# A hybrid decoder step on one Trainium2 core: u laid out by transfers inside the chip in stage 1, the state recurrence on GpSimd

## The chip, the cores and the metric

The kernel runs on one core of a Trainium2 chip. A core has TensorE (PE: matrix products and transposes, into PSUM), VectorE (DVE), ScalarE (ACT), GpSimd (POOL) and SyncE (SP); each runs its own list of instructions and waits for the others by semaphores. SyncE, ScalarE and GpSimd can issue transfers (DMA). The metric is the device time of the kernel in microseconds.

## The reference, cut to what matters

One step of a one-layer decoder on 256 prompt tokens and 8 x 8 sample tokens (NT = 320), width 2048. It has an attention branch, a state space branch (S5) with 64 groups of 16 channels and 64 complex states, gates that merge them, and a feed-forward part. What bears on the change:

```python
z = _rmsnorm(x, g_mix) @ w_in                       # columns: q 1024, kv 1536, gt 48, u 1024, mg 4096
# the S5 branch, per group of 16 channels of u
xr = jnp.einsum('btgc,gpc->btgp', uf, bbr)
xi = jnp.einsum('btgc,gpc->btgp', uf, bbi)
# h[t] = a * h[t-1] + x[t], a and h complex, started with h0 for the samples and 0 for the prompt
_, _, hr, hi = lax.associative_scan(_cplx_affine_combine, (a_r, a_i, xr, xi), axis=1)
y = (jnp.einsum('btgp,gcp->btgc', hr, c_re) - jnp.einsum('btgp,gcp->btgc', hi, c_im)
     + d_skip.reshape(SSM_NGROUPS, SSM_GROUP) * uf)
```

All is float32. The large products are made of three: each operand is split into a rounded part (hi) and the rest (lo), and hi x hi, hi x lo and lo x hi are added.

## The kernel before, in words

The kernel is a row of programs, each a list for every engine, with a barrier between them (`program`, L141).

**Stage 1** (L377 to L595) makes q, kv, gt and u. Weights come in tiles of 128 columns (1 MB): SyncE loads (`load_tile`, L231), ScalarE rounds (`round_tile`, L245), VectorE subtracts (`rest_tile`, L252), TensorE multiplies (`multiply`, L259, 48 matmuls of 320 columns), and VectorE scales the result into its place (`scale_in`, L555). The order is q (8 tiles), kv (12), gt (one, in two halves), u (8). GpSimd only loads a few small tables (L400 to L409). `uT` has channels on partitions and tokens along a row, and lies in `oT`.

**Stage 2** (L764 to L1241) is the S5 branch, with time cut into chunks of L = 8 tokens: 40 chunks, 32 of the prompt and 8 of the samples. Between its pieces lie the *dense steps*, the function `D` of each engine (L647 to L703): half a tile (8 blocks of 128 rows) of the gate columns mg, 24 matmuls on TensorE, with a load and a rounding on ScalarE (L629), a subtraction on VectorE (L633) and, every second time, a scaled copy out (`gate_out`, L641) and its store. 48 of them belong to this stage. `half_load` n reuses one of three buffers, rounding n one of two, so ScalarE may round step n + 1 when TensorE has finished step n − 1. By hand, TensorE's order is:

1. 24 transposes of u (L854), their copies to `un` (VectorE L1065, ScalarE L990), three stores to DRAM (`u_dram`, L778) and loads back as rows of chunks (L784). SyncE and ScalarE issue the parameter loads before (L769 to L774, L985 to L995).
2. 9 dense steps, between which VectorE makes the powers of a (L1110 to L1122), Bbar (L1127 to L1132) and the copies of C and h0 (L1139, L1142). Small transposes stand between them (L860, L869, L878).
3. The pair loop over 32 pairs of groups (L914): `spread_pair` on VectorE (L1147) makes `EB` for pair m + 3; GpSimd copies u of one pair (L828); `turn_pair` transposes EB (L894) and u (L896); ScalarE copies both (L1014, L1015); `multiply_pair` (L907) makes the chunk inputs `ea`, which VectorE copies (L1166). A dense step after every second pair. At m = 12 and 20 VectorE builds a table Q (`make_q`, L1169).
4. `taps` of parts 0 and 1 (L934), whose results ScalarE copies (`keep_taps`), and 8 dense steps, while VectorE runs the recurrence: `state_step` (L1208), five small operations, 31 times for the 31 chunk borders, and then the final states. TensorE waits for `h_done` (L965).
5. Eight parts of four pairs: `outputs_of` (L949, L956), two dense steps, `taps(part + 2)`. VectorE makes Q for part + 2 between its two dense steps. GpSimd adds the diagonal (L840, L845); SyncE then spreads the taps into a block matrix T by eight transfers inside the chip (`spread_g`, L787), which `outputs_of` reads, and stores the outputs. T must have been cleared by GpSimd (L832).
6. The final states are transposed and stored (L977, L978).

The stages behind (attention with the last 8 gate tiles, samples, merge and feed-forward) are not touched, but for where a few buffers lie.

## Time and profile before

| | us |
|---|---|
| three runs | 2180.3, 2175.05, 2174.73 |
| median | 2175.05 |
| the profiled execution | 2175.88 |
| its span, first to last instruction | 2174.1 |

In that execution TensorE is busy for 2053.7 us (94%), VectorE for 1071.0 (49%), ScalarE for 799.9 (37%) and GpSimd for 114.7 (5%). The busy time of TensorE is modelled for its pipelined matmuls, so a full stretch is not proof of full use, but an empty one is proof of the opposite. Its clock, where nothing lowers it, is 2.4 GHz, shown as 1.00; the mean of the span is 0.977. In a row of the trace the number in front is the start in microseconds from the start of the span, the second the duration, and brackets hold the idle time of that engine before the operation and what ended it.

### The profile page before, as it was taken

The page shows a single profiled execution, that of the slowest core. Times are in us where ns is not written, and L with a number is a line of the kernel's source. Part 1 is how long each engine was busy: PE and PEld are TensorE (multiplying, and loading weights), DVE is VectorE, ACT ScalarE, POOL GpSimd, SP SyncE. Part 2 cuts the span into 40 slices and gives each one's busy share as a digit, 9 for nine tenths or more (in the row PEclk, how much of TensorE's full clock was granted, in tenths as well). Part 3 has the DMA queues.
Part 4 walks back from the last instruction along what each step waited for, and adds up shares of the span by engine and source line. Part 5 has one row for each costly group of instructions (what it writes and reads, how often), then busy time and mean ns, then how long its engine had stood idle before and what let it go on. Part 6 is the DMA issues. An engine that isn't in the chain of part 4 may idle for free.

```text
span 2174.1 us, 39080 instructions
## 1 busy us (share of the span) xinstructions
PE 2053.7 (94%) x15964; PEld 1924.6 (89%) x15964; DVE 1071.0 (49%) x1725; ACT 799.9 (37%) x1132; POOL 114.7 (5%) x173
## 2 busy tenths in 40 slices
PE   8999798898897888899999999999999999999997
PEld 6999787787885555599999999999999999999996
DVE  4433487774563344545554444444444444444443
ACT  5222232343343455654434333223322333233344
POOL 1000011000000212200001000000000000000011
PEclk9999898999997999999999999999999999999999
DMA  7645543455356988745645445455545554554443
GB/s 184 201 135 155 136 123 98 124 147 155 90 162 252 375 313 330 284 151 172 213 139 153 142 148 155 133 160 152 154 132 158 155 149 128 154 168 144 140 134 115
DMA packets 554452, 364.74 MB, mean 168 GB/s; under 512 B 68913, under 2 KB 529666, under 8 KB 553506
## 3 DMA queue, kind: packets, MB, share of 16 engines
q1 hardware_dynamic: 472530, 314.00, 47.0%
q10 hardware_dynamic: 80096, 41.25, 7.1%
q0 software_dynamic: 1712, 7.97, 1.1%
q8 instruction: 72, 1.18, 0.2%
q14 instruction: 42, 0.34, 0.0%
HBM read 345.45 MB, written 23.63 MB: 170 GB/s over the span
## 4 chain that ended last, share of the span: by engine, by line
PE 56%; issue 6%; SPq 2%; DMA 1%; DVE 1%; ACT 1%; POOL 1%; POOLq 0%; DVEq 0%; ACTq 0%
PE bank L279 55%; SPq L1284 1%; SPq L1285 1%; DMA arena<-in_cache_kv_dram 0%; POOL ysT L1733 0%; DMA xT<-out_dram 0%; DVE w_lo L255 0%; PE bank L1866 0%; PE bank L1841 0%; ACT w_hi L250 0%; PE bank L2082 0%; PE bank L1832 0%; POOL arena L1743 0%; DVE rstd L2596 0%; PE bank L1800 0%
## 5 line engine op out<-in xcount | busy, mean ns | idle before, releaser
L279 PE MATMUL bank<-hx,w_hi 128*128 128x320 f32 x3072 | 676.3, 309 | 1.5 <-DVE w_lo L255 1.5
L255 DVE TENSOR_TENSOR w_lo<-w_raw,w_hi 128x2048 fp32r<-128x2048 f32 (+2 forms) x222 | 464.0, 2090 | 345.6 <-ACT w_hi L250 345.5
L279 PE MATMUL bank<-act,w_hi 128*128 128x320 f32 x2432 | 537.0, 310 | 3.2 <-DVE w_lo L255 2.4
L279 PEld LDWEIGHTS bank<-hx,w_hi 128*128 128x128 f32 x3072 | 513.8, 188 | 1.9 <-issue 1.8
L250 ACT CAST w_hi<-w_raw 128x2048 fp32r<-128x2048 f32 (+2 forms) x222 | 385.5, 1737 | 318.3 <-PE bank L279 314.4
L279 PE MATMUL bank<-hx,w_lo 128*128 128x320 f32 x1536 | 474.6, 309 | 0.0
L279 PEld LDWEIGHTS bank<-act,w_hi 128*128 128x128 f32 x2432 | 406.0, 188 | 4.6 <-DVE w_lo L255 3.1
L279 PE MATMUL bank<-act,w_lo 128*128 128x320 f32 x1216 | 375.8, 309 | 0.0
L279 PEld LDWEIGHTS bank<-hx,w_lo 128*128 128x128 f32 x1536 | 288.3, 188 | 0.0
L662 PE MATMUL bank<-actr,half_hi 128*128 128x320 f32 x1024 | 239.9, 323 | 20.6 <-DVE half_lo L633 20.3
L279 PEld LDWEIGHTS bank<-act,w_lo 128*128 128x128 f32 x1216 | 228.3, 188 | 0.0
L662 PEld LDWEIGHTS bank<-actr,half_hi 128*128 128x128 f32 x1024 | 176.5, 196 | 28.6 <-DVE half_lo L633 25.9
L279 PE MATMUL bank<-actr,w_hi 128*128 128x320 f32 x896 | 197.4, 309 | 1.2 <-DVE arena L565 1.2
L662 PE MATMUL bank<-actr,half_lo 128*128 128x320 f32 x512 | 162.1, 317 | 0.0
L279 PEld LDWEIGHTS bank<-actr,w_hi 128*128 128x128 f32 x896 | 149.9, 188 | 1.6 <-DVE arena L565 1.5
L279 PE MATMUL bank<-actr,w_lo 128*128 128x320 f32 x448 | 138.4, 309 | 0.0
L633 DVE TENSOR_TENSOR half_lo<-half_raw,half_hi 128x1024 fp32r<-128x1024 f32 x64 | 78.1, 1220 | 66.5 <-ACT half_hi L629 66.2
L629 ACT CAST half_hi<-half_raw 128x1024 fp32r<-128x1024 f32 x64 | 66.8, 1045 | 119.3 <-PE bank L662 70.5
L2329 ACT CAST act<-arena 128x320 fp32r<-128x320 f32 x44 | 20.2, 459 | 231.0 <-DVE arena L2612 231.0
L662 PEld LDWEIGHTS bank<-actr,half_lo 128*128 128x128 f32 x512 | 100.0, 195 | 0.0
L2326 ACT ACTIVATE cst<-arena 128x320 f32<-128x320 f32 x44 | 20.8, 472 | 191.2 <-DVEq L2604 191.2
L279 PEld LDWEIGHTS bank<-actr,w_lo 128*128 128x128 f32 x448 | 84.1, 188 | 0.0
(395 smaller groups left out, 1777.2 us busy)
## 6 DMA issues: line engine op xcount, KB each, us to landing
arena<-in_cache_kv_dram SPq DMA_DIRECT2D x120, 512.0 KB, 7.1
w_raw<-in_w_gate_dram SPq DMA_DIRECT2D x44, 1024.0 KB, 5.1
w_raw<-in_w_up_dram SPq DMA_DIRECT2D x44, 1024.0 KB, 5.1
w_raw<-in_w_down_dram SPq DMA_DIRECT2D x64, 704.0 KB, 4.7
half_raw<-in_w_in_dram ACTq DMA_DIRECT2D x64, 512.0 KB, 4.5
w_raw<-in_w_in_dram SPq DMA_DIRECT2D x20, 1024.0 KB, 5.1
w_raw<-in_w_glu_dram SPq DMA_DIRECT2D x32, 512.0 KB, 5.0
w_raw<-in_w_out_dram SPq DMA_DIRECT2D x16, 1024.0 KB, 5.8
```

Of the source, the lines that this page charges most:

```text
L250: nc.scalar.copy(w_hi[s][:, 0:job.kt * job.width], raw[s][:, 0:job.kt * job.width]).then_inc(S(f"hi_ready{s}"), 1)
L255: nc.vector.tensor_tensor(w_lo[s][:, 0:job.kt * job.width], raw[s][:, 0:job.kt * job.width], w_hi[s][:, 0:job.kt * job.width].bitcast(F32) ...
L279: mm = pe.matmul(bank[:, 0:NT], w[s][:, at:at + P], x[:, kk, :], start=first and k == 0 and m == 0, stop=final and k == job.kt - 1 and m == 2)
L629: nc.scalar.copy(half_hi[n % 2][:, :], raw3[n % 3][:, :]).then_inc(S("w_rounded"), 1)
L633: nc.vector.tensor_tensor(half_lo[n % 2][:, :], raw3[n % 3][:, :], half_hi[n % 2][:, :].bitcast(F32), ALU.subtract).then_inc(S("w_split"), 1)
L662: mm = pe.matmul(PS[t % 2][:, 0:NT], w[h][:, k * P:(k + 1) * P], actr[:, x, 8 * h + k, :], start=h == 0 and k == 0 and m == 0, stop=h == 1 ...
L1284: at = sp.value_load(ptab[0:1, n:n + 1], min_val=0, max_val=n_pool - 1)
L1285: sp.dma_start(dst, page_rows[bass.ds(at, 1), :, :].rearrange("o t n -> (o t) n")).then_inc(S(landed), 16)
L2326: A.activation(sB[0], tg, ACT.Silu).then_inc(S("silu_ready"), 1)
L2329: A.copy(actr[:, 0, i, :], tmp).then_inc(S("hid_rounded"), 1)
```

## The change

- In stage 1 u comes before kv and gt. Its scaled copy puts the tokens of a chunk position together (`u_in`). When u is complete, GpSimd issues 64 transfers from `uT` to `UTa_flat` (now in `ysT`), 16 partitions x 8 x 40 elements each. The transposes of u, `un`, the stores and loads by `u_dram`, GpSimd's copies (L828), the transposes at L896 and the copies at L1014 are gone.
- The first three half loads and all parameter loads of stage 2 are issued at the end of stage 1, and waited for there.
- In stage 2 the small transposes come first, six dense steps precede the pair loop (of these, VectorE handles three between the first three `spread_pair`). ScalarE makes the copies of C and h0. The powers are made in three rounds of 1, 2 and 4; Bbar for 8 pairs before the loop, for 24 at its start.
- In the pair loop ScalarE copies the products (`copy_pair`), two pairs late.
- The recurrence is on GpSimd (`scan_steps`), for 16 pairs at a time: all 31 steps of the first half from pair 16 of the loop on, the second half in pieces of 11, 11 and 9 steps behind the diagonals of parts 1, 2 and 3. TensorE waits for `h_done` before part 0 and before part 4.
- Dense steps: 6, then 16 in the loop, 4 before the parts, and 3, 3, 3, 3, 3, 3, 2, 2 in the parts (`PART_D`).
- The final states of the samples are made on VectorE in part 2.

```diff
-                for n, job in enumerate((job_q[1], job_kv, job_gt, job_u)):
+                for n, job in enumerate((job_q[1], job_u, job_gt, job_kv)):
...
+                for n in range(3):
+                    half_load(sp, gates, n)
...
+                taps_in = UTa_flat.rearrange("p (t g h a) -> p t g h a", t=8, g=4, h=2)
+                for j in range(8):
+                    for s in range(L):
+                        pool.dma_start(taps_in[s * CH:(s + 1) * CH, :, j // 2, j % 2, :],
+                                       uT[j * CH:(j + 1) * CH, :, s * NCH:(s + 1) * NCH]).then_inc(S("u_spread"), 16)
+                pool.wait_ge(S("u_spread"), 64 * 16)
...
-                for m in range(GH):
-                    part = m // PG
-                    if m % PG == 0:
-                        pool.wait_ge(S(f"u_landed{part % 2}"), 16 * (part // 2 + 1))
...
+                def scan_steps(half, first, last):
+
+                    gs = slice(half * HG, (half + 1) * HG)
+                    a8r = PK[:, 0, L, gs].unsqueeze(1).broadcast_to([P, 2, HG])
+                    for n in range(first, last):
+                        state, extra = Ha[:, n, :, gs], ea[:, n, :, gs]
+                        G.tensor_tensor(sc[:, 1, 0, gs], NPI[:, L, gs], state[:, 1, :], ALU.mult)
+                        G.tensor_tensor(sc[:, 1, 1, gs], PK[:, 1, L, gs], state[:, 0, :], ALU.mult)
+                        scan_link(G.tensor_tensor(sc[:, 0, :, gs], a8r, state, ALU.mult))
+                        scan_link(G.tensor_tensor(sc[:, 2, :, gs], sc[:, 0, :, gs], extra, ALU.add))
+                        out = Ha[:, n + 1, :, gs] if n < SCAN else FinP[:, :, gs]
+                        scan_link(G.tensor_tensor(out, sc[:, 2, :, gs], sc[:, 1, :, gs], ALU.add))
+
+                pool.wait_ge(S("h_zero"), 1)
+                pool.wait_ge(S("powers_ready"), 1)
+                pool.wait_ge(S("e_copied"), HG)
+                scan_steps(0, 0, SCAN)
+                pool.sem_inc(S("h_done"), 1)
                 pool.wait_ge(S("eb_ready"), GH)
                 for b in range(2):
                     nc.gpsimd.memset(Tt[b], 0.0).then_inc(S("t_zero"), 1)
...
+                    if part == 1:
+                        pool.wait_ge(S("e_copied"), GH)
+                    if 1 <= part < 4:
+                        scan_steps(1, STEPS[part], STEPS[part + 1])
...
-                for _ in range(8):
+                for _ in range(4):
                     D()
-                pe.wait_ge(S("h_done"), 1)
                 for part in range(NPART):
+                    if part % 4 == 0:
+                        pe.wait_ge(S("h_done"), part // 4 + 1)
                     outputs_of(part)
-                    D()
-                    D()
+                    for _ in range(PART_D[part]):
+                        D()
...
-                    nc.scalar.copy(UTa[:, m, :], PS[4 + m % 2][:, 256:336])
                     nc.scalar.copy(stg[m % 2], PS[4 + m % 2][:, 0:256]).then_inc(S("e_staged"), 1)
+                    if m >= 2:
+                        copy_pair(m - 2)
                     if m % 2:
                         D()
...
                 for part in range(NPART):
-                    D()
-                    if part + 2 < NPART:
-                        make_q(part + 2)
-                    D()
+                    for n in range(PART_D[part]):
+                        D()
+                        if n == 0 and part + 2 < NPART:
+                            make_q(part + 2)
```

## Rows read from the trace of the kernel before

**Rows 1.** Stages by time: busy us of each engine, clock, DMA share, GB/s.
```profile
236.40:290.50 54.10, 42.48 (x264) 40.48 (x265) 36.52 (x122) 15.43 (x19) 0.77 (x2) 0.87 0.76 184
290.50:389.10 98.60, 91.50 (x746) 81.75 (x744) 71.86 (x187) 30.79 (x80) 16.66 (x34) 0.91 0.40 108
389.10:438.00 48.90, 38.66 (x330) 35.02 (x330) 41.92 (x180) 13.41 (x28) 1.98 (x6) 1.00 0.44 116
438.00:511.50 73.50, 72.31 (x832) 64.78 (x836) 47.51 (x63) 32.74 (x88) 5.36 (x16) 1.00 0.58 149
```

**Rows 2.** TensorE in order of time, start of stage 2: start, duration, operation, idle before.
```profile
236.49 4.04 PE L854 MATMUL bank<-cst,oT 128*128 128x128 f32 x20 [2.36 <-PEq L148]
...
249.32 0.90 PE L662 MATMUL bank<-actr,half_hi 128*128 128x320 f32 x2 [4.46 <-DVE half_lo L633]
```

**Rows 3.** VectorE in order of time, around the parameter chain.
```profile
256.71 0.25 DVE L1073 COPY xT<-bank 128x96 f32<-128x96 f32 x1
...
263.21 0.49 DVE L641 TENSOR_TENSOR sq<-bank,rstd 128x320 f32<-128x320 f32 x1
```

**Rows 4.** TensorE in order of time, one turn of the pair loop.
```profile
310.92 0.38 PE L894 MATMUL bank<-cst,ysT 128*128 128x128 f32 x2
311.24 0.31 PE L896 MATMUL bank<-cst,arena 40*128 40x40 f32 x2
311.48 0.44 PE L907 MATMUL bank<-arena,ysT 128*64 128x40 f32 x8
...
312.83 0.56 PE L662 MATMUL bank<-actr,half_hi 128*128 128x320 f32 x2
...
316.45 0.38 PE L894 MATMUL bank<-cst,ysT 128*128 128x128 f32 x2
```

**Rows 5.** VectorE's groups in stage 2: operation, count, busy us, mean ns, idle before.
```profile
L633 DVE TENSOR_TENSOR half_lo<-half_raw,half_hi 128x1024 fp32r<-128x1024 f32 x48 | 58.5, 1218 | 33.4 <-ACT half_hi L629 33.1 <-DVE oT L1230 0.2
L1158 DVE TENSOR_TENSOR arena<-arena 128x256 f32<-128x256 f32 x32 | 13.9, 434 | 0.0
L641 DVE TENSOR_TENSOR sq<-bank,rstd 128x320 f32<-128x320 f32 x24 | 11.6, 484 | 7.6 <-PE bank L662 7.4
...
L1186 DVE TENSOR_TENSOR oT<-arena 128x576 f32<-128x576 f32 x8 | 6.4, 802 | 0.0
...
L1139 DVE COPY arena<-bank 64x256 f32<-64x256 f32 x8 | 3.4, 421 | 0.1
```

**Rows 6.** TensorE's waits from 392 to 438: us in total, times, longest.
```profile
PE bank L662 <- DVE half_lo L633: 8.9, 6, 1.7
```

**Rows 7.** VectorE and GpSimd in order of time, 291 to 294.
```profile
291.18 1.08 POOL L828 COPY arena<-arena 40x256 f32<-40x256 f32 x2 [31.86 <-PE bank L896]
...
291.93 0.61 DVE L1158 TENSOR_TENSOR arena<-arena 128x256 f32<-128x256 f32 x1
```

**Rows 8.** GpSimd's operations: L828 (min/median/max ns), and two lines in order of time.
```profile
L828 POOL COPY arena<-arena x32: 393/419/720, 258.6 to 379.0; 40x256 f32<-40x256 f32 x32
...
449.41 0.45 POOL L845 TENSOR_TENSOR arena<-arena,oT 16x128 f32<-16x128 f32 x1 [50.41 <-ACT arena L1028]
449.94 0.53 POOL L840 TENSOR_TENSOR oT<-cst,ysT 16x64 f32<-16x64 f32 x2
```

**Rows 9.** TensorE and VectorE in order of time, one part.
```profile
457.04 1.06 PE L934 MATMUL bank<-arena 64*16 64x128 f32 x32
...
467.79 1.06 PE L934 MATMUL bank<-arena 64*16 64x128 f32 x32
...
463.27 0.75 DVE L1185 TENSOR_TENSOR arena<-arena 128x576 f32<-128x576 f32 x1
...
468.05 1.22 DVE L633 TENSOR_TENSOR half_lo<-half_raw,half_hi 128x1024 fp32r<-128x1024 f32 x1
```

**Rows 10.** GpSimd's transfers and ScalarE's last rounding in stage 1; ScalarE's B loads.
```profile
37.16 1.19 POOL L408 DMA_DIRECT2D phi<-in_w_cmp_phi_dram  x2
...
218.68 1.91 ACT L250 CAST w_hi<-w_raw 128x2048 fp32r<-128x2048 f32 x1 [5.19 <-PE bank L279]
...
248.97 5.48 ACTq L994 DMA_DIRECT2D xT<-in_ssm_b_im_dram  x2
```

More of the change, by code:

```diff
@@ L360, in build @@
         uT = oT
+        UTa_flat = ysT[:, :, :].rearrange("p k n -> p (k n)")
+        with ExitStack() as alias:
+            alias.enter_context(nc.sbuf_tensor("w1_place", [P, 6 * KT * P], F32))
+            raw3 = [alias.enter_context(nc.sbuf_tensor(f"half_raw{r}", [P, 8 * P], F32)) for r in range(3)]
+            state_par = alias.enter_context(nc.sbuf_tensor("state_par", [P, 2560], F32))
         phase = ExitStack()
@@ L375, in build, with __init__, half_load @@
         HALF = DM // 2
+        MG_S5 = 24
+        MG_ALL = 32
+        class Gates:
+            def __init__(self, t0, tiles, early=False):
+                self.t0, self.n, self.early = t0, 2 * tiles, early
+        def half_load(eng, gates, n):
+            ahead = gates.early and n < 3
+            if n >= 3:
+                eng.wait_ge(S("w_split"), n - 2)
+            col = C_MG + (gates.t0 + n // 2) * P
+            eng.dma_start(raw3[n % 3][:, :].rearrange("p (k c) -> p k c", k=8),
+                          w_in[(n % 2) * 1024:(n % 2 + 1) * 1024, col:col + P].rearrange("(k p) c -> p k c", p=P))\
+                .then_inc(S(f"half_early{n}" if ahead else f"w_landed{n % 3}"), 16)
+        par = state_par[:, :]
+        Cn = par[:, 0:2048].rearrange("p (r t d s) -> p r t d s", r=2, t=8, d=2)
+        dcol = par[:, 2304:2304 + 2 * GH].rearrange("p (h g) -> p h g", h=2)
+        par = xT[:, :, :].rearrange("p k n -> p (k n)")
+        h0n = par[:, 0:512].rearrange("p (r t n) -> p r t n", r=2, t=2)
+        lamn = par[:, 512:896].rearrange("p (a n) -> p a n", a=3)
+        ldn = par[:, 896:898]
+        Bn = par[:, 1024:2048].rearrange("p (r g c) -> p r g c", r=2, g=GH)
+        tp = par[:, 2048:2560].rearrange("p (t g) -> p t g", t=16)
+        gates = Gates(0, MG_S5, early=True)
         with program() as block:
@@ L409, in _ @@
                 pool.wait_ge(S("phi_landed"), 32)
+                for s in range(2):
+                    pool.wait_ge(S(f"bank_free{s}"), job_u.base + job_u.n + 1)
+                taps_in = UTa_flat.rearrange("p (t g h a) -> p t g h a", t=8, g=4, h=2)
[4 more added lines that the diff above has]
+                pool.wait_ge(S("u_spread"), 64 * 16)
             @block.tensor
@@ L710, in build @@
         take = scratch()
-        urows = [take(L * PG * 32).rearrange("p (s c) -> p s c", s=L) for _ in range(2)]
-        QT_flat = take(2 * 2 * PG * 9 * CH + 2 * 2 * PG * P)
+        take_m = scratch(mid[:, :], 8192)
+        urows = [take_m(L * PG * 32).rearrange("p (s c) -> p s c", s=L) for _ in range(2)]
+        QT_flat = take_m(2 * 2 * PG * 9 * CH + 2 * 2 * PG * P)
         take_q = scratch(QT_flat, 2 * 2 * PG * 9 * CH + 2 * 2 * PG * P)
@@ L725, in build @@
         RK = take(2 * GH * L).rearrange("p (r g s) -> p r g s", r=2, g=GH)
-        H0 = take(2 * NB * GH).rearrange("p (r b g) -> p r b g", r=2, b=NB)
-        FinP = take(2 * GH).rearrange("p (r g) -> p r g", r=2)
-        ust = [take(256).rearrange("p (h s c) -> p h s c", h=2, s=L) for _ in range(2)]
-        sc = take(3 * 2 * GH).rearrange("p (t r g) -> p t r g", t=3, r=2)
         tAB_flat = Tt[1].rearrange("p h g n -> p (h g n)")
@@ L845, in _ @@
                     nc.gpsimd.tensor_tensor(Ga[part % 2][0:CH, :, :, 0:CH], Ga[part % 2][0:CH, :, :, 0:CH], dI[0:CH], ALU.add).then_inc(S("g_diag"), 1)
+                    if part == 1:
+                        pool.wait_ge(S("e_copied"), GH)
+                    if 1 <= part < 4:
+                        scan_steps(1, STEPS[part], STEPS[part + 1])
+                    if part == 3:
+                        pool.sem_inc(S("h_done"), 1)
+                        for half in range(2):
+                            scan_steps(half, SCAN, SCAN + 1)
+                        pool.sem_inc(S("fin_ready"), 1)
             @block.tensor
             def _(pe):
[L849 to L857 removed]
                 pe.wait_ge(S("ldt_rows"), 1)
@@ L879, in _ @@
                 tr.then_inc(S("h0_full"), 1)
-                D()
-                D()
-                D()
+                D = dense_pe(pe, gates)
+                for _ in range(6):
+                    D()
                 pe.wait_ge(S("ct_ready"), 1)
@@ L1032, in _ @@
                 keep_taps(1)
-                for _ in range(8):
+                for _ in range(4):
                     D()
@@ L1044, in _ @@
                         ins.then_inc(S("y_copied"), 1)
-                    D()
-                    D()
+                    for _ in range(PART_D[part]):
+                        D()
                     if part + 2 < NPART:
@@ L1226, in _ @@
[L1226 to L1236 removed]
+                for _ in range(4):
+                    D()
```

301 lines of the change are left out of this document (125 added, 176 removed).

## The prediction

> **What bounds the kernel now.** I read first the table of stages, then the waits of TensorE inside each, then the other engines beside them. A *dense step* below is one half tile of the gate projection, 24 matmuls that have nothing to do with the state space branch and are dealt out between its pieces to keep TensorE busy. There are 48 of them, 9 + 16 + 8 + 15 by place, and they need no more than 3.6 us each. In [rows 1] TensorE is nearly always busy only in the last stretch. In the first, 54.1 us hold 9 dense steps and a few transposes, 42.5 us of busy time, part of it at the lower clock (mean 0.87). In the pair loop 98.6 us hold 91.5 busy. In the third, 48.9 hold 38.7: the recurrence runs on VectorE, which also has to split the weights of the dense steps. So the stage is bound by TensorE's work plus about 45 us of gaps and slow clock, and only what closes a gap, or takes TensorE work away, is worth anything.
>
> The gaps: TensorE begins the stage at 236.49, and its first dense step at 249.32, because the transposes of u, their copies and the parameter loads come first; that step starts at the lower of the clock's two levels, 1.2 GHz [rows 1, 2]. In the pair loop TensorE repeats every 5.53 us (310.92 to 316.45 in [rows 4]) with no gap: 1.91 us for two pairs, 3.62 for a dense step; so there TensorE is the limit [rows 4]. Sixteen such turns are 88.5 us; the other 10 of the 98.6 us lie around the two tables (make_q) that VectorE builds inside the loop. In the recurrence the dense steps wait 8.9 us in all for VectorE [rows 6].
>
> **The change part by part.** Every time is of the profiled execution, 2175.88 us with a span of 2174.1, 0.8 us above the median 2175.05 of the three runs; the sum is made against it.
>
> *Transposes of u, the round trip through DRAM, the parameter loads.* They leave the start of the stage. TensorE then has 23 small transposes (4.4 us by the 4.04 us of 20, [rows 2]) and goes into its first dense step at about 241.1 in place of 249.3. Its second step needs what is split by 239.9 (round 1.05, then two splits of 1.2 [rows 5]), so steps 1 and 2 run to 248.1. Then the parameter chain holds both helpers. It is 256.71 to 263.21 now with a split of 1.2 in it [rows 3], so 5.8 without, 240.1 to 245.9. ScalarE has its sines by 243.4, copies C and H0 (nine copies, 3.4 us, as eight take VectorE 8 x 0.42 [rows 5]) and rounds until 248.0, so step 3 is split at 249.2: 1.1 us idle. VectorE goes on with the last powers (three rounds in place of seven; 1.3), tables (1.6), one quarter of Bbar (1.4), a gate copy (0.4) and a split: step 4 at 255.0, 2.3 idle after 252.7. Steps 5 and 6 need their splits at 257.8 and 261.2 and run from 258.5 and 262.0 without a gap; pairs begin at 265.6: 29.1 us for 6 steps in place of 54.0 for 9. **−24.9 us.** The bounds are −28 (no idle time) and −20 (idle as now, and the lower clock again after it).
>
> *Pair loop.* The two 40-column transposes of u leave TensorE: each pair of them takes 0.24 us (311.24 to 311.48 [rows 4]), 32 times 7.7 us, so a turn of two pairs takes 5.04. VectorE gives its copy of the pair's result to ScalarE, and has 3.8 us of work in 5.04 (two spreads of 1.2, a split of 1.2; half of a 0.4 us gate copy [rows 5]). The copy on ScalarE waits for the same product as the copy to `stg` behind it did; queued behind it are that stage and the next rounding, which are not due for another 3 us. make_q (six operations like L1186, 4.6 us in all [rows 5]) now hits a VectorE that no longer waits for TensorE's products, and whose lead is worth about 2.9 us of it: 1.7 us of idle time each time, twice, for about 5. A late fourth pair at the loop's start costs 1.4, ScalarE's order some 1. 15 dense steps and 32 pairs: 77.5 + 5.8 = 83.3 for 98.6. **−15.3 us**, bounds −20 (no stall) and −11 (stalls as now, less the transposes).
>
> *Between the loop and the parts.* The recurrence leaves VectorE, 4 dense steps in place of 8 stand here, and TensorE waits for `h_done` behind them, with all later work queued behind that wait. One step, the taps (3.45 us as now, with ScalarE's copies between them), 4 steps, 0.7 for a load that is late, and the outputs of part 0 (2.4): 24.4 us for 48.9. **−24.5 us**, if GpSimd is in time. One half step of the recurrence on GpSimd is five operations of 16 or 32 elements. It has none like it in this trace. A 16x64 operation and its successor take 0.53 us, a 16x128 one 0.45, and a dependent one starts 0.07 us after the one before ends (449.41 + 0.45 to 449.94 [rows 8]); on that line 16 elements cost 0.16 us and 32 cost 0.20, and the half step 0.13 + 0.13 + 0.20 + 2 x 0.20 + 3 x 0.07 = 1.07 us. It may start when pair 15 is copied, at about 307.5, so 31 steps end at 341. Behind it wait the two clears of T (1.9), the diagonal of part 0 (1.0) and SyncE's eight spreading transfers with their landing (about 8). TensorE asks for part 0 at about 371. The scan is hidden while a half step costs less than (371 − 307.5 − 10.9)/31 = 1.7 us. I take 1.1. The upper bound is 2.0, by the longest against the usual L828 copy (720 and 419 ns [rows 8]) on every instruction: 9 us more. The lower bound is nothing, since it is hidden.
>
> What speaks against this edit: VectorE and GpSimd slow each other. VectorE's 128x256 product, 0.43 us on average [rows 5], took 0.61 at 291.93 [rows 7] while L828 ran on GpSimd. That is rival 3. A rule of the Trainium skill stands behind it (GPSIMD Engine Reference, Key points): GpSimd shares its SBUF interfaces with VectorE, and contends above all with operations that have two SBUF inputs. By that rule both engines' operations in the second half of the loop are such ones; the row agrees.
>
> *Second half, in parts 1 to 3.* 11 steps take 12 us of a part's 14 to 15.5, and GpSimd adds the next diagonal in the rest. Final state and `h_done` 2 come at about 411; part 4 asks for it at 430. Hidden up to about 1.3 us a step; above it part 3 is late by the difference.
>
> *The parts.* They have 22 dense steps in place of 15: 7 x 3.52 = 24.6 us more in a stretch that is full. And one thing that is not free. A part takes 10.75 us now (457.04 to 467.79), the rounding and split that precede make_q end at its start, 463.27, and the split behind it runs to 469.2 [rows 9]. That is harmless now, as this split is for the next part. The third dense step of the new part wants it at 467.5, when the second ends: 1.6 us idle in each of the six parts that still build tables, 9.6 us; bounds 0 and 14 (the tables stretched as in rival 3 in parts 1 to 3). Waits of 1.3 to 1.7 us have not lowered the clock in the recurrence, where it is 1.00 [rows 1, 6]. **+34.2 us.**
>
> *Stage 1.* u before kv changes no total. GpSimd issues 64 transfers of 20 KB; those of 128 runs that it issues now take 0.6 us each [rows 10], so 38 us, beside gt and twelve tiles of kv, 13 x 7.04 = 91.5 us. 0. At the end of the stage ScalarE is free from 220.6 (218.68 + 1.91 [rows 10]) and issues the B tables, which took it 2.7 us each in the crowd at 249 (5.48 for two [rows 10]): at most 220.6 + 1.5 + 11 + 6 to land = 239, at the least 230, where the next stage begins at 236.49 now [rows 2]. I take 0, bounds 0 and +4.
>
> **Sum.** −24.9 − 15.3 − 24.5 + 34.2 = −30.5 us. 2175.9 − 30.5 = 2145 us. The end of the stage, with its final transposes, and all later stages stay as they are.
>
> **Rivals.**
> 1. *The table on VectorE costs the parts nothing*, since ScalarE's rounding comes earlier than I put it: 9.6 us better, 2136. For it: the parts wait for nothing now. Against it: the split ends at 469.2 in [rows 9].
> 2. *GpSimd is late*: at 2.0 us a half step part 0 waits 9 us, 2154, and parts 3 and 4 some 3 more. For it: the trace has no such operation; L828 spreads from 393 to 720 ns [rows 8]. Against it: a dependent one starts after 0.07 us.
> 3. *The shared interface*: VectorE's 3.8 us in the pair loop become 5.5 at 0.61/0.42, more than 5.04, 0.5 us a turn for seven turns, and the tables of parts 1 to 3 take 2 us longer each: 9.5 us, 2155. Against it: on the line above, the elements make only 0.04 to 0.08 of the 0.16 to 0.20 us of such an operation, so it should touch the tiles for less than half of its time (an estimate).
> 4. *Slower than before*: the 64 transfers of GpSimd are not issued at 0.6 us. From 91.5/64 = 1.43 us they lengthen stage 1, from (91.5 + 30.5)/64 = 1.9 us they eat the gain, and at 2.5 us the time is 2175.9 + 160 − 122 = 2214. For it: the row has only two in succession, and ScalarE's took 2.7 us in a crowd [rows 10]. By a fit in the Trainium skill (DMA: Bandwidth & Descriptors, Anatomy of one DMA) such a transfer takes about 2.0 us; end to end that would be 131 us, 39 more than the window and 2184 us. No row shows them one after the other to the landing, and the semaphore is waited for once, at the end.
> 5. *The change gives nothing*, TensorE's gaps turn up elsewhere: 2175.
>
> **How the numbers follow.** Forecast 0.47 (2140 to 2150 by its own bounds), rival 1 0.17, rival 2 0.15, rival 3 0.13, rival 4 0.05, rival 5 0.03. The range 2133 to 2157 takes in the first four cases and leaves out the last two and the far ends of the others. 0.3% (6.5 us) is about what a measurement of this kernel can tell from no change: faster 0.92, same 0.03, slower 0.05.
>
> **What would show it.** In the new profile: first dense step at about 241; two-pair turn 5.0 us; 23 to 30 us between the loop's last product and the first outputs; the scan's operations at 0.16 to 0.20 us and its end before 350; in the parts a wait of TensorE for `half_lo` of 1.3 to 1.7 us before each third dense step, a period of 15.4 to 16; the last u transfer landed before 190. It is wrong if TensorE waits at `h_done`, if VectorE's operations are longer during the scan, or if stage 1 ends after 239.

## The result and the profile after

The changed kernel takes 2171.44 us (median of 18 runs, 2162.42 to 2176.74); the kernel before, beside it, 2177.8. The ratio is 0.9969, 95% interval 0.9957 to 0.998: faster by 0.31%, where 1.4% was forecast (2145 us, range 2133 to 2157). The sign was right, the size was not, and the time lies outside the range. The profiled execution took 2164.37 us with a span of 2162.6, 7.1 us less than the median; what follows is read from it.

Lines have moved: a dense step is L727 on TensorE (L662 before), its split L698 (L633), the gate copy L706, the outputs L987, the taps L972, the diagonal on GpSimd L896, its transfers by SyncE L830, the recurrence L871 to L876.

First, the parts of the forecast that came true. Stages by time of the changed kernel (busy us of PE, PEld, DVE, ACT, POOL; clock, DMA share, GB/s):

```profile
236.00:265.50 29.50, 25.70 (x168) 25.11 (x169) 24.32 (x89) 13.92 (x22) 0.00 (x0) 0.94 0.37 101
265.50:349.40 83.90, 79.03 (x683) 71.38 (x680) 67.63 (x155) 30.74 (x78) 37.47 (x103) 0.98 0.44 117
```

The pairs begin at 265.5 (265.6 forecast) and the loop's last product ends at 349.4 (348.9 forecast), 39.7 us ahead of the kernel before. The two stretches that [rows 1] showed as 54 and 99 us are 29.5 and 84. The 64 transfers of u are one row of GpSimd:

```profile
141.06 33.34 POOL L467 DMA_DIRECT2D ysT<-oT  x64 [102.80 <-DVE oT L635]
```

They are issued in 33 us, 0.52 us each, and TensorE's first operation of stage 2 starts at 236.87, for 236.49 in [rows 2]. The gain so far is 40 us. At the next stage, which starts at 515.28 for 524.25 before, only 9.0 us are left; the stages behind take 2.5 us less in this execution. So 31 us are given back between 349.4 and 515.3, where 9.7 were forecast.

This trace starts stage 2 early. In the traces of the experiments below, which share stage 1 with it, that first operation comes at 237.06 once (experiment 2) and at 240.3 to 242.3 nine times. The 3.4 us and more are lost long before u is moved: from 20 to 40 us TensorE begins 116 matmuls in this trace and 84 to 93 in those nine. From the start of stage 2 to the loop's end it is 112.6 us here and 111 to 115 in the experiments (108.4 in experiment 3, with its shorter split), for 152.6 in the kernel before, so the 40 us gained in the stage are no accident. The kernel before has one trace, with 115 matmuls from 20 to 40 us; whether its other executions start late as well is not shown.

TensorE's waits from 350 to 510 in the changed kernel (us in total, times, longest):

```profile
PE bank L727 <- DVE half_lo L698: 7.8, 6, 1.7
PE bank L987 <- DMA mid<-mid: 6.9, 1, 6.9
PE bank L987 <- DMA mid<-oT: 5.5, 2, 5.0
PE bank L987 <- issue: 4.5, 1, 4.5
```

The first row is the wait before each third dense step, forecast at 9.6 us and 7.8 in fact. The other three are new: the outputs of parts 0, 3 and 4 wait 6.9, 5.0 and 4.5 us. What they wait for is seen by setting three rows of GpSimd and three of TensorE beside each other:

```profile
370.52 0.45 POOL L896 TENSOR_TENSOR mid<-mid,oT 16x128 f32<-16x128 f32 x1
...
424.93 0.52 POOL L896 TENSOR_TENSOR oT<-oT 16x128 f32<-16x128 f32 x1
...
446.86 1.32 POOL L896 TENSOR_TENSOR mid<-mid,oT 16x128 f32<-16x128 f32 x1
...
378.06 1.08 PE L987 MATMUL bank<-mid,ysT 128*40 128x128 f32 x8 [6.89 <-DMA mid<-mid]
...
432.58 1.08 PE L987 MATMUL bank<-mid,ysT 128*40 128x128 f32 x8 [5.00 <-DMA mid<-oT]
...
454.99 0.97 PE L987 MATMUL bank<-mid,ysT 128*40 128x128 f32 x8 [4.53 <-issue]
```

From the end of each diagonal (L896) to the outputs are 7.1, 7.1 and 6.8 us: SyncE's eight transfers to T and their landing. `h_done` is never what is late. GpSimd makes the diagonals, and it makes them behind its pieces of the recurrence. The first half starts at 307.16 (307.5 forecast) and ends at 367.5, not at 341: 31 half steps in 60.3 us, 1.95 us each, where 1.07 was taken and 2.0 was the upper bound. GpSimd's groups from 305 to 372:

```profile
L871 POOL TENSOR_TENSOR mid<-arena,xT 128x16 f32<-128x16 f32 x31 | 12.1, 392 | 135.1 <-ACT xT L1043 132.8
L873 POOL TENSOR_TENSOR mid<-arena,xT 128x32 f32<-128x32 f32 x31 | 11.5, 370 | 0.0
```

A mean of 0.37 to 0.39 us, and for 16 elements more than for 32: that is no price of an operation but a mixture. In order of time, GpSimd and then VectorE:

```profile
357.79 0.22 POOL L871 TENSOR_TENSOR mid<-arena,xT 128x16 f32<-128x16 f32 x1
...
358.15 0.25 POOL L873 TENSOR_TENSOR mid<-arena,xT 128x32 f32<-128x32 f32 x1
...
359.14 1.23 POOL L871 TENSOR_TENSOR mid<-arena,xT 128x16 f32<-128x16 f32 x1
...
361.86 1.30 POOL L873 TENSOR_TENSOR mid<-arena,xT 128x32 f32<-128x32 f32 x1
...
364.25 0.25 POOL L873 TENSOR_TENSOR mid<-arena,xT 128x32 f32<-128x32 f32 x1
...
359.06 1.23 DVE L698 TENSOR_TENSOR half_lo<-half_raw,half_hi 128x1024 fp32r<-128x1024 f32 x1 [5.35 <-ACT half_hi L694]
361.82 1.23 DVE L698 TENSOR_TENSOR half_lo<-half_raw,half_hi 128x1024 fp32r<-128x1024 f32 x1 [1.53 <-ACT half_hi L694]
364.16 0.49 DVE L706 TENSOR_TENSOR sq<-bank,rstd 128x320 f32<-128x320 f32 x1 [1.12 <-PE bank L727]
```

While VectorE is idle the operations take 0.22 and 0.25 us, and a step repeats every 1.35 us (355.10, 356.44, 357.79). The operation that meets a split stands until the split ends (359.14 + 1.23 = 360.37 beside 359.06 + 1.23 = 360.29). Beside the gate copy L706, one input of which comes from PSUM, it takes its usual 0.25, as do the others of the half that begin beside a gate copy (0.22 or 0.25). In the first half 11 operations stand beside the 11 splits that begin in it, one beside each, 13.3 us for what is 2.6 alone. Of the 60.3 us, 31 x 1.34 = 41.5 are the recurrence by itself and 18.8 are standing, 10.7 beside the splits and the rest beside the spreads and the tables. The reverse hardly shows: in the same stretch VectorE's split takes 1.235 us on average beside the recurrence and 1.221 without it (experiment 1 below), its two products for the spreads 0.44 to 0.46 and 0.42.

Behind a long wait there is a second loss. Stages of the changed kernel behind the first outputs, the same columns as above:

```profile
378.00:380.00 2.00, 1.94 (x24) 1.34 (x24) 0.00 (x0) 0.00 (x0) 1.61 (x8) 0.50 0.57 90
...
384.00:386.00 2.00, 2.00 (x16) 2.00 (x15) 2.00 (x3) 0.00 (x0) 1.92 (x4) 1.00 1.00 269
...
378.00:395.60 17.60, 16.72 (x154) 14.55 (x154) 8.47 (x10) 4.26 (x9) 13.60 (x35) 0.84 0.56 135
...
472.00:488.00 16.00, 14.42 (x157) 13.07 (x152) 8.76 (x11) 6.08 (x16) 0.98 (x3) 1.00 0.55 139
```

The clock is at 0.50, 1.2 GHz, right behind the wait and back at 1.00 by 384. The same work, three dense steps and a table, takes 16.72 us of busy time in part 0 and 14.42 in part 5: 2.3 us for each of the first two waits, 1.4 for the third.

### The profile page after: what moved, and what is told of

Same layout as the page of the kernel before. It is cut to its first block, busy times and chain, and to the rows that moved or that the text cites. A ratio compares the mean times of both kernels' runs of the same rounds, so it can differ in the third digit from the quotient of the medians.

```text
span 2162.6 us, 39026 instructions
## 1 busy us (share of the span) xinstructions
PE 2041.7 (94%) x15876; PEld 1916.6 (89%) x15876; DVE 1034.7 (48%) x1503; ACT 801.4 (37%) x1138; POOL 249.1 (12%) x525
## 4 chain that ended last, share of the span: by engine, by line
PE 57%; issue 6%; ACT 1%; SPq 1%; DVE 1%; DMA 1%; POOL 1%; POOLq 0%; DVEq 0%; ACTq 0%
PE bank L278 55%; SPq L1295 0%; PE bank L1877 0%; SPq L1296 0%; POOL ysT L1744 0%; DMA xT<-out_dram 0%; DVE w_lo L254 0%; DMA arena<-in_cache_kv_dram 0%; PE bank L1852 0%; PE bank L1820 0%; PE bank L1811 0%; PE bank L1843 0%; ACT w_hi L249 0%; PE bank L1921 0%; PE bank L2093 0%
## 5 line engine op out<-in xcount | busy, mean ns | idle before, releaser
L727 PE MATMUL bank<-actr,half_hi 128*128 128x320 f32 x1024 | 236.0, 319 | 13.1 <-DVE half_lo L698 13.1
L727 PEld LDWEIGHTS bank<-actr,half_hi 128*128 128x128 f32 x1024 | 173.5, 192 | 20.5 <-DVE half_lo L698 17.0
L727 PE MATMUL bank<-actr,half_lo 128*128 128x320 f32 x512 | 160.5, 313 | 0.0
L698 DVE TENSOR_TENSOR half_lo<-half_raw,half_hi 128x1024 fp32r<-128x1024 f32 x64 | 78.7, 1230 | 122.9 <-ACT half_hi L694 122.9
L727 PEld LDWEIGHTS bank<-actr,half_lo 128*128 128x128 f32 x512 | 98.4, 192 | 0.0
```

The source lines that it names most:

```text
L698: nc.vector.tensor_tensor(half_lo[n % 2][:, :], raw3[n % 3][:, :], half_hi[n % 2][:, :].bitcast(F32), ALU.subtract).then_inc(S("w_split"), 1)
L727: mm = pe.matmul(PS[t % 2][:, 0:NT], w[h][:, k * P:(k + 1) * P], actr[:, x, 8 * h + k, :], start=h == 0 and k == 0 and m == 0, stop=h == 1 ...
```

## The experiments

One length is compared throughout, since it depends neither on when stage 2 began nor on what the clock did earlier in it: from the end of the pair loop's last product to the first product of the next stage (36 of 128x128, x20 and x16 in the kernel before). There is one trace of each kernel, so one length. In the kernel before:

```profile
388.43 0.69 PE L907 MATMUL bank<-arena,ysT 128*64 128x40 f32 x16
...
524.25 3.68 PE L1387 MATMUL bank<-cst,kvT 128*128 128x128 f32 x20 [5.72 <-PEq L148]
```

524.25 − 389.12 = 135.1 us, with 23 dense steps in it. The forecast made of it 135.1 − 24.5 + 34.2 = 144.8, with 26 steps.

| kernel | loop ends | first outputs | next stage | length | ratio, 95% |
|---|---|---|---|---|---|
| before | 389.12 | 435.43 | 524.25 | 135.1 | |
| changed | 349.42 | 378.06 | 515.28 | 165.9 | 0.9969 (0.9957 to 0.998) |
| 1, recurrence on VectorE | 355.49 | 401.81 | 504.58 | 149.1 | 0.9894 (0.9876 to 0.9912) |
| 2, half the recurrence | 349.65 | 371.38 | 496.40 | 146.8 | 0.9881 (0.9859 to 0.9903) |
| 3, split with one input | 349.37 | 373.08 | 503.54 | 154.2 | one time, 2154.02 us |
| 4, tables later | 354.22 | 383.76 | 517.46 | 163.2 | 0.9964 (0.9949 to 0.9978) |
| 5, three operations | 354.14 | 375.94 | 502.78 | 148.6 | 0.9862 (0.9839 to 0.9885) |
| 6, three and tables later | 354.16 | 375.97 | 500.93 | 146.8 | 0.9861 (0.9834 to 0.9888) |
| 7, three, on VectorE | 352.14 | 395.14 | 499.03 | 146.9 | 0.9871 (0.9851 to 0.9891) |
| 8, six steps ahead | 354.60 | 384.22 | 510.68 | 156.1 | 0.991 (0.9886 to 0.9933) |
| 9, GpSimd's order | 356.37 | 385.02 | 513.52 | 157.2 | 0.9938 (0.9911 to 0.9965) |
| 10, as 6, and GpSimd's order | 351.76 | 373.56 | 488.58 | 136.8 | 0.9853 (0.9823 to 0.9883) |

**1. The recurrence back on VectorE.** All else of the change stays; 18 dense steps in the parts.

```diff
-        PART_D = (3, 3, 3, 3, 3, 3, 2, 2)
+        PART_D = (3, 3, 2, 2, 2, 2, 2, 2)
...
-                for _ in range(4):
+                for _ in range(8):
...
+                for n in range(SCAN):
+                    state_step(Ha[:, n], ea[:, n], Ha[:, n + 1])
+                    if n % 4 == 3:
+                        D()
```

> The recurrence goes back to VectorE, whole width, between the pair loop and the parts, with 8 dense steps there and 18 in the parts (3, 3, 2, 2, 2, 2, 2, 2); u inside the chip and the shorter start of stage 2 stay. The changed kernel's loop ends 39.7 us earlier than the kernel before (349.4 against 389.1). Theory 1 (the recurrence on GpSimd is what eats the gain): the rest of the stage runs as before, plus 3 dense steps of 3.52 us and two waits of 1.6 us = 13.8, so the next stage begins at 524.3 - 39.7 + 13.8 = 498 where the changed kernel has 515.3; some 2147 us, ratio 0.987. Rival (the gain is lost in the parts, whoever runs the recurrence, by the lower clock and waits for the split): the next stage begins at 511 to 516, ratio 0.996 to 0.997. No wait of TensorE for T or h_done above 2 us by theory 1.

Measured: 149.1 us, where theory 1 works out to 135.1 + 13.8 = 148.9, and the ratio 0.9894. The next stage begins at 504.6 and not at 498, since the loop itself ended 6.1 us later: 3.6 us from a later start of stage 2 (240.51 for 236.87) and 2.4 in it, where the clock was 0.88 and not 0.94 between 236 and 265.5. So all of the change but the recurrence on GpSimd is worth 1.1%, and that half takes 0.75% of it away.

**2. Half the recurrence.**

```diff
-        STEPS = (0, 0, 11, 22, SCAN)
+        STEPS = (0, 0, 5, 10, 15)
...
-                scan_steps(0, 0, SCAN)
+                scan_steps(0, 0, 15)
```

> Left out: 16 of the 31 steps of the recurrence in each half, and so the states behind them; all else is the changed kernel. What GpSimd's lateness costs is measured by itself. Theory 1 (three waits of 6.9, 5.5 and 4.5 us, and the lower clock behind them, are the loss): half 0 ends at 307 + 15 x 1.95 = 336, the three waits are gone, outputs of part 0 at about 370 in place of 378, next stage at 493 to 497 in place of 515.3, time 2143 to 2147, ratio 0.985 to 0.987. Rival (the waits hide others; TensorE would wait for VectorE's splits instead): next stage above 505, ratio over 0.992.

The steps behind the 15th, and so the states that need them, are left out. Measured: the three waits are gone, outputs of part 0 at 371.38 (371 in the prediction), length 146.8, 2 us above the 144.8 forecast. GpSimd's lateness costs 19 us of the 21 that are missing. Waits from 350 to 495 in this kernel:

```profile
PE bank L727 <- DVE half_lo L698: 9.1, 6, 2.0
```

9.1 us is the term of 9.6. Behind the longest of these waits, 1.95 us before 430.57, the clock is at 0.50 again; such a fall costs 1.7 us in experiment 9, which would be most of the 2 us. The ratio by several runs, 0.9881, is short of the expected 0.985 to 0.987.

**3. A split with one input.**

```diff
-            nc.vector.tensor_tensor(half_lo[n % 2][:, :], raw3[n % 3][:, :], half_hi[n % 2][:, :].bitcast(F32), ALU.subtract)
+            nc.vector.tensor_scalar(half_lo[n % 2][:, :], raw3[n % 3][:, :], 0.5, None, ALU.mult)
```

> The split of the gate weights on VectorE is a product with a constant: one input of SBUF where the changed kernel subtracts one tile of SBUF from another. So the lower half of the split is not what the reference wants. Theory 1 (an operation of GpSimd stands while VectorE works on two inputs of SBUF): the recurrence's operations of 0.9 to 1.3 us that begin beside a split are gone (21 of them now), those beside the tables (0.7 to 0.8) stay, and the first half ends 6 to 9 us earlier, at 358 to 361 in place of 367.5. Rival (any long operation of VectorE on SBUF holds GpSimd): the operations beside the split last as long as the new operation itself, and all of them are still there. Second rival (GpSimd's operations are this slow by themselves, 0.35 us on average): the end moves by less than 2 us.

The subtraction is left out, and its result is wrong by that. Measured: the first half ends at 362.6, 4.9 us earlier, though it began 2.6 later: it takes 52.8 us for 60.3. The time, measured once, is 2154.02 us. But the standing is not gone. VectorE, then GpSimd:

```profile
318.84 0.69 DVE L698 TENSOR_SCALAR half_lo<-half_raw 128x1024 fp32r<-128x1024 f32 x1 [1.56 <-ACT half_hi L694]
...
319.00 0.64 POOL L874 TENSOR_TENSOR mid<-mid,xT 128x32 f32<-128x32 f32 x1
```

Ten operations of the half take 0.55 to 0.69 us beside the new operation of 0.68 to 0.80. Theory 1's "two inputs" falls, and the first rival holds: an operation of GpSimd stands until VectorE's ends, beside the subtraction with two inputs from SBUF and beside this product with one, but not beside the gate copy, which has one input from SBUF and one from PSUM. The size of the loss follows the duration of VectorE's instruction. The product is a fast form, 0.7 us for the same 1024 elements that take the subtraction 1.23; a slower one with one input was not run. The Trainium skill (SBUF — State Buffer, sections SBUF: two separate sides and Who interferes with whom) says just that: the two engines have one pair of ports in common, taken for a whole instruction, and the other engine is blocked fully and not slowed; a product with a constant in its faster mode takes the pair too. The trace agrees, by 0.64 us here and 1.23 above.

**4. Tables later.**

```diff
-                        if n == 0 and part + 2 < NPART:
+                        if n == 1 and part + 2 < NPART:
```

> In each part the table on VectorE is built after the second dense step's split in place of after the first's. Theory 1 (the third step waits since the table stands before its split; but parts 3 and 4 wait for GpSimd, whatever VectorE does): the 10.7 us of waits for the split are gone, of which those in parts 0 to 3 come back at parts 3 and 4, where the waits for GpSimd grow from 5.5 and 4.5 us to about 8 each; gain 3 to 5 us, next stage at 510 to 512, ratio 0.9945 to 0.9955. Rival (these waits add up with the others): 9 to 11 us, ratio 0.992. Rival (the wait moves to the first step of the next part): no gain, ratio 0.9965 to 0.997.

Measured: length 163.2, 2.6 us less; by the runs it can't be told from the changed kernel. The waits from 350 to 515:

```profile
PE bank L987 <- DMA mid<-oT: 8.8, 2, 7.4
PE bank L987 <- DMA mid<-mid: 7.8, 1, 7.8
PE bank L987 <- issue: 4.8, 1, 4.8
...
PE bank L727 <- DVE half_lo L698: 0.4, 1, 0.4
```

The 7.8 us of waits for the split are 0.4 and the waits for T have grown from 16.9 to 21.4. More than half of what was saved at the split is waited away at T, as theory 1 has it, with a gain slightly under its 3 to 5 us. Where it comes back is not as it says: parts 0, 3 and 4 wait 7.8, 7.4 and 4.8 us for 6.9, 5.0 and 4.5, so part 4 has none of it.

**5. Three operations a half step.** All four products in one operation, from a table of a8 in four places; then two sums.

```diff
-                        G.tensor_tensor(sc[:, 1, 0, gs], NPI[:, L, gs], state[:, 1, :], ALU.mult)
-                        G.tensor_tensor(sc[:, 1, 1, gs], PK[:, 1, L, gs], state[:, 0, :], ALU.mult)
-                        scan_link(G.tensor_tensor(sc[:, 0, :, gs], a8r, state, ALU.mult))
+                        scan_link(G.tensor_tensor(sc[:, 0:2, :, gs], T8[:, :, :, gs], state.unsqueeze(2).broadcast_to([P, 2, 2, HG]), ALU.mult))
```

> The recurrence on GpSimd as in the changed kernel, but with three operations a half step in place of five: one product of 64 elements (all four products, from a table of a8 in four places), then two sums of 32. With VectorE idle the five operations start 0.18, 0.18, 0.33, 0.33 and 0.32 us apart, 1.34 us a step; three would take about 0.35 + 0.33 + 0.33 = 1.0. The 60.3 us of the first half are 41.5 by that and 18.8 of standing beside VectorE. Theory 1 (GpSimd stands for a fixed share of the time, 18.8/60.3): 31 us / 0.69 = 45, so the half ends at 352 and not at 367.5, the waits of 6.9, 5.5 and 4.5 us are gone or under 1, and the time is that of the short recurrence, ratio 0.985 to 0.989. Rival (an operation on GpSimd costs by its elements): step above 1.7 us, half ends after 360, part 0 waits, ratio 0.992 or more.

Measured: a step takes 1.06 us beside an idle VectorE, and the product of 64 elements 0.33, where 16 take 0.22:

```profile
352.45 0.33 POOL L871 TENSOR_TENSOR mid<-arena,xT 128x64 f32<-128x64 f32 x1
352.86 0.25 POOL L872 TENSOR_TENSOR mid<-mid,xT 128x32 f32<-128x32 f32 x1
353.19 0.25 POOL L874 TENSOR_TENSOR xT<-mid 128x32 f32<-128x32 f32 x1
353.51 0.32 POOL L871 TENSOR_TENSOR mid<-arena,xT 128x64 f32<-128x64 f32 x1
```

The half takes 46.3 us (313.3 to 359.6), 1.49 a step, near the 45 of theory 1, and the waits for T are down to one of 1.0: 148.6 us, ratio 0.9862. Eight splits begin in the half and eight operations stand beside them. So an operation is held by each split here too, 8 of 8 as 11 of 11 before; there are fewer because the half is shorter. This is the smallest edit here that gets the forecast gain.

**6. Three operations, and tables later.** The edits of 4 and 5 together; the table for both:

```diff
+                for c in range(2):
+                    G.tensor_copy(T8[:, c, c, :], PK[:, 0, L, :])
+                G.tensor_copy(T8[:, 0, 1, :], PK[:, 1, L, :])
+                scan_link(G.tensor_copy(T8[:, 1, 0, :], NPI[:, L, :]))
```

> Three operations a half step on GpSimd, and the table of each part after the second dense step's split. Theory 1 (with GpSimd in time the 10 to 12 us of waits for the split add up with what is gained, where alone they only gave way to waits for GpSimd): 8 to 10 us below the kernel with three operations alone, loop's last product to next stage 137 to 139 us (165.9 in the changed kernel, 146.8 with the short recurrence), ratio 0.980 to 0.984. Rival (parts of 14 to 14.5 us are shorter than the 11 steps, diagonal and transfers that GpSimd has in each, so parts 3 and 4 wait again, 2 to 5 us each): 142 to 147 us, ratio 0.984 to 0.987.

Measured: 146.8, the rival's figure. The split's waits are 0.2 us, but part 4 waits 7.3 for T: its diagonal stands behind the last piece of the recurrence and the final states, and ends at 435.5.

**7. Three operations, on VectorE.** Against experiment 1:

```diff
-                    V.tensor_tensor(sc[:, 0], a8r, state, ALU.mult)
-                    V.tensor_tensor(sc[:, 1, 0, :], NPI[:, L, :], state[:, 1, :], ALU.mult)
-                    link(V.tensor_tensor(sc[:, 1, 1, :], PK[:, 1, L, :], state[:, 0, :], ALU.mult))
+                    link(V.tensor_tensor(sc[:, 0:2], T8, state.unsqueeze(2).broadcast_to([P, 2, 2, GH]), ALU.mult))
```

> The recurrence on VectorE, whole width, after the loop (8 dense steps there, 18 in the parts), with three operations a step. With five a step takes 0.97 us; three would take about 0.3 + 0.26 + 0.26 = 0.8, so 31 steps 5 us less. Theory 1 (VectorE is what this stretch waits for): loop's last product to next stage 144 us in place of 149.1, ratio 0.986 to 0.988. Rival (ScalarE's rounding and the order of splits decide; VectorE waits 8.0 us for it there): 148 to 149, ratio 0.989 to 0.990.

Measured: a step every 0.85 us (0.97 with five), length 146.9: 2.2 us less than in experiment 1, between the theory's 5 and nothing. The 31 steps are 3.7 us shorter, and from the loop's end to the first outputs it is 3.3 us less (43.0 for 46.3). VectorE's waits for ScalarE's rounding there stay as they were (7.4 us, 7.3 with five), so they are not what eats the rest: 1.1 us is lost again in the parts, where the outputs wait 2.3 us for T in place of 1.2. With three operations a step the runs don't tell the recurrence on VectorE (0.9871) from that on GpSimd (0.9862).

**8. Six dense steps ahead of the parts.**

```diff
-        PART_D = (3, 3, 3, 3, 3, 3, 2, 2)
+        PART_D = (3, 3, 3, 3, 2, 2, 2, 2)
...
-                for _ in range(4):
+                for _ in range(6):
```

> The changed kernel with two dense steps moved from parts 4 and 5 to before part 0: 6 there, and 3, 3, 3, 3, 2, 2, 2, 2 in the parts. Theory 1 (three waits for GpSimd at fixed points of time): outputs of part 0 still at 378, without a wait, those of parts 3 and 4 still at about 432 and 455, and behind them two dense steps and two waits for the split less, 7.0 + 3.2 us: next stage at 505 in place of 515.3, ratio 0.991 to 0.993. Rival (the later outputs push GpSimd's second half back): gain below 4 us, ratio over 0.995.

Measured: 156.1, 9.8 us less (10.2 expected), ratio 0.991. Part 0 waits 0.8 us, parts 3 and 4 wait 4.3 and 5.3. This agrees with theory 1.

**9. GpSimd's order alone.**

```diff
-        STEPS = (0, 0, 11, 22, SCAN)
+        STEPS = (0, 0, 15, 23, SCAN)
...
                         pool.sem_inc(S("h_done"), 1)
+                    if part == 4:
                         for half in range(2):
                             scan_steps(half, SCAN, SCAN + 1)
```

> The changed kernel with nothing but GpSimd's order of work altered: of the second half 15, 8 and 8 steps in parts 1, 2 and 3 in place of 11, 11 and 9, and the last state of both halves behind the diagonal of part 4 in place of ahead of it. In the changed kernel part 3 and part 4 wait for T, whose eight transfers start behind the diagonal (424.93 to outputs at 432.58, 446.86 to 454.99: 7.7 and 8.1 us), and h_done is no wait. Theory 1 (the diagonals queued behind the recurrence on GpSimd make parts 3 and 4 late): diagonal of part 3 at 418 and of part 4 at 435, T in time for both, 5.5 + 4.5 us and two stretches at the lower clock of some 1.7 us gone: loop's last product to next stage 152 to 154 us (165.9 in the changed kernel), ratio 0.990 to 0.992. Part 0 still waits 6 to 7 us. Rival (the second half itself is too late and h_done takes the place): part 4 waits 4 us or more, 157 to 162 us, ratio 0.993 to 0.996.

Measured: the waits of parts 3 and 4 are gone and part 0's is as before, as theory 1 says, and no wait for `h_done` takes their place; but the length is 157.2 and not 152 to 154, and the ratio, 0.9938, lies in the rival's range. Waits from 350 to 510:

```profile
PE bank L727 <- DVE half_lo L698: 9.0, 6, 2.0
PE bank L988 <- DMA mid<-mid: 6.9, 1, 6.9
```

The waits for the split are 1.2 us longer than in the changed kernel, and the rest of what is missing is again the clock, now behind these waits. TensorE at one of these waits, and the clock (third number from the end) before it, behind it, and in two whole parts:

```profile
430.13 0.56 PE L727 MATMUL bank<-actr,half_hi 128*128 128x320 f32 x2 [1.80 <-DVE half_lo L698]
...
424.00:428.00 4.00, 4.00 (x29) 4.00 (x28) 3.93 (x6) 1.05 (x1) 3.84 (x6) 1.00 1.09 316
...
432.00:434.00 2.00, 2.00 (x9) 2.00 (x8) 1.90 (x6) 0.00 (x0) 1.77 (x6) 0.50 0.31 71
...
402.50:418.60 16.10, 14.37 (x156) 13.05 (x152) 8.98 (x11) 6.05 (x16) 14.44 (x38) 1.00 0.53 137
418.60:436.40 17.80, 16.00 (x158) 14.63 (x154) 12.10 (x18) 6.13 (x17) 16.02 (x40) 0.90 0.52 134
```

A part with such a fall takes 17.8 us for 16.1, and there are two. In the parts of all traces here, the five with waits for the split of 1.80 to 2.01 us had a fall (experiments 2, 5 and 9), and those with shorter ones, up to 1.73, didn't. But the length of one wait does not decide it. In the pair loop of the kernel before, the clock falls right behind a wait of 1.49 us:

```profile
362.42 0.41 PE L894 MATMUL bank<-cst,ysT 128*128 128x128 f32 x2 [1.49 <-issue]
...
358.00:360.00 2.00, 2.00 (x16) 2.00 (x15) 1.93 (x4) 0.00 (x0) 0.00 (x0) 1.00 0.76 190
364.00:366.00 2.00, 0.89 (x4) 0.58 (x4) 1.93 (x8) 0.00 (x0) 0.00 (x0) 0.50 0.00 0
```

In experiment 1 it falls behind one of 1.64 us, before 274.02; behind one of 1.65 in experiment 4, before 275.16, it doesn't. What decides it is open.

**10. Experiment 6 with GpSimd's order mended** (the final states behind part 4's diagonal, as in 9).

```diff
-        STEPS = (0, 0, 11, 22, SCAN)
+        STEPS = (0, 0, 19, 26, SCAN)
```

> Three operations a half step on GpSimd, each part's table after the second dense step, and GpSimd's order altered: 19, 7 and 5 steps of the second half in parts 1, 2 and 3, the last states behind part 4's diagonal. Theory 1 (the last wait, 7.3 us for T of part 4 and the lower clock behind it, is all that stands between 146.8 us and the kernel without waits for GpSimd or the split): loop's last product to next stage 136 to 139 us, outputs every 14.1 to 14.4 us, ratio 0.981 to 0.984, faster than all others. Rival (TensorE then waits for the tables or for VectorE's splits): 142 us or more, ratio over 0.9845.

Measured: 136.8 us, as theory 1 says. The largest waits from 350 to 486:

```profile
PE bank L975 <- DVE mid L1218: 2.1, 4, 0.6
PE bank L975 <- ACT mid L1071: 1.2, 2, 0.8
```

A part takes 14.3 to 14.9 us at a clock of 1.00. The median of the four runs is 2144.01 us, the ratio 0.9853, above the expected 0.981 to 0.984 and in the rival's range. It beats both kernels: 27 us less than the changed kernel, whose length here was 29 us more. The trace is of the fastest of the four, 2132.82 us, 10.9 less than the next, so the slower ones may hold waits that it doesn't show. From experiments 5 and 6, both at 0.986, its runs don't part it; the trace does, by 10 to 12 us.

## Why the prediction was wrong

Step by step, against its own terms:

- *Start of the stage*, −24.9: right. Pairs begin at 265.5; the waits before the third and the fourth dense step are 0.7 and 2.2 us, forecast 1.1 and 2.3.
- *Pair loop*, −15.3: right, 83.9 us for 83.3. VectorE, which rival 3 had slowed to 5.5 us a turn, is hardly slowed (0.44 to 0.46 us for 0.42).
- *Stage 1*, 0: right in this trace, 0.4 us late, and rival 4 is out: 0.52 us a transfer. In nine of the experiments' traces stage 2 starts 3.4 to 5.4 us later, which is lost before the transfers and was no term of the sum.
- *Between the loop and the parts*, −24.5: **the step that failed.** It said that GpSimd's 31 half steps end at 341 and are hidden under 1.7 us a step. The price had two faults. The operations by themselves cost 0.22 and 0.25 us and not 0.13 to 0.20 (a step of 1.34 for 1.07, 8 us of the half); I had taken them from operations on 16 partitions and pulled a fixed share out of two shapes [rows 8]. That alone would have been hidden: 307.2 + 41.5 = 348.7. The other 18.8 us are the standing beside VectorE. The forecast had seen the shared interface, and looked for it on the wrong engine and in the wrong size: [rows 7] showed a VectorE operation 0.2 us longer, so I made VectorE the victim, and argued that small operations touch the tiles too seldom to matter. But a blocked operation waits for the end of the other's instruction, however small it is itself, and it is the small ones that have much to lose. The row that said so was in [rows 8], L828 with 720 ns at most for a usual 419: both copies of 720 ns, at 335.38 and 363.14, began during a split. It was read as the spread of a price, and used only for an upper bound of 2.0 us. That the measured 1.95 lies so near is luck: 1.07 x 720/419 is 1.84, and a per cent on every instruction is not what happens. Of the signs that the prediction names, the end of the scan before 350 is the one that caught it.
- *Second half, in parts 1 to 3*, hidden up to 1.3 us a step: wrong by the same price. The pieces of 11 steps took 20.6 and 25.1 us, 1.9 and 2.3 a step, where 12 us were forecast. Above its limit it had part 3 late; that part 4 would be late by its diagonal, which stands behind the last piece and the final states (7.4 us), and not by `h_done` 2, it didn't say. Between the first two pieces GpSimd stands idle for 4.4 us, since the diagonal of part 2, at 397.63, waits for a copy of ScalarE; experiment 9 fills that time with steps. It shows that the order is the cause of both waits by moving nothing else.
- *The parts*, +34.2: right as to the wait before the third dense step (7.8 us for 9.6). "Waits of 1.3 to 1.7 us have not lowered the clock" was true of the recurrence, and holds for these waits in the changed kernel too (up to 1.73); but the pair loop of the same trace has a fall behind one of 1.49, and in experiments 2, 5 and 9 some of these waits are 1.8 to 2.0 and have one.

The sum again, for the length of 165.9 us: 144.8 forecast; + 16.4 for the waits of 6.9, 5.0 and 4.5 us; + 6.0 for the low clock behind them (2.3 + 2.3 + 1.4); − 1.8 for the third steps, 7.8 in place of 9.6. That is 165.4, and 0.5 is open. With the 0.5 us by which the loop ended late and the 2.5 us less behind the stage these 21.1 us make the traced 2164.4 from the forecast 2145. The other 7.1 us up to the median are in no trace of this kernel; a later start of stage 2 would explain them in part, which is not shown.

Rival 2 (GpSimd late, 2.0 us a step) was the true case, and rival 3's mechanism was its cause. I had them as two cases and gave each its own price. Rival 2's own, 9 us at part 0 and 3 at the others, 2154, was too low: part 0 cost 9.2 with its clock, parts 3 and 4 together 13.2. It came near for part 0 by luck, since 2.3 of the 9.2 are the clock, which it left out; for the others it left out the clock and the diagonal of part 4.

## What to carry to other kernels

When small dependent operations are moved to GpSimd beside a busy VectorE, add up the durations of VectorE's instructions on SBUF that they will meet, one meeting each, and not a slowdown in per cent. A shorter chain meets fewer of them, so what an operation less saves counts more than its own time (14.0 us of the half for 31 x 0.28 = 8.7). Of the work on that engine's queue ask what else stands behind it: here a 0.45 us diagonal, with 7 us of transfers behind it, was what TensorE waited for, and a change of order freed it. A long wait of TensorE is priced with the stretch at the lower clock that follows.

## What the runs showed of the hardware

- An operation of GpSimd on SBUF that begins beside one of these VectorE instructions stands until it ends: 1.11 to 1.30 us beside a split of 1.23, 0.55 to 0.69 beside a product with a constant of 0.7 to 0.8, nothing beside an operation with an input from PSUM (0.25 us).
- On GpSimd alone, 128 partitions: 16 elements 0.22 us, 32 elements 0.25, 64 elements 0.33; the next dependent operation starts about 0.08 us after the end. On VectorE 0.18 us for 32 elements, 0.22 for 64 and 0.29 for 128.
- 64 transfers on GpSimd's queue were issued in 33.34 us, 0.52 each. Eight by SyncE inside the chip have landed 7 us after their data is there.
- In the parts, behind waits of TensorE of 1.80 us and more the granted clock was 0.50 for some 3 to 6 us; behind those up to 1.73 it stayed at 1.00. In the pair loop it was 0.50 behind one of 1.49 (kernel before) and one of 1.64 (experiment 1), and 1.00 behind one of 1.65 (experiment 4).
